# Feed-forwards: the sums of squares over the features as two products of 128 columns

## The chip, the core and the metric

One core of a Trainium2 chip. The metric is the device time of one execution in microseconds (us), median over several executions. Engines are named as in the profile: PE is TensorE's matmul, PEld its weight load, DVE is VectorE, ACT is ScalarE, POOL is GpSimd, SP is the engine that issues the DMAs.

## What is computed

Two layers of an encoder block and then two layers of a hybrid attention block, on one sequence of 256 tokens with 1024 features. Each encoder layer is a feed-forward, a mixer (stick-breaking attention beside a gated delta rule), a cross attention on a memory of 256 tokens, and a second feed-forward. All in float32.

```python
def rms_norm(x, gain, eps=RMS_EPS):
    xf = x.astype(F32)
    y = xf * lax.rsqrt(jnp.mean(xf * xf, axis=-1, keepdims=True) + eps)
    return (y * gain.astype(F32)).astype(x.dtype)

def swiglu_ffn(x, w_in, w_out):
    gate, up = jnp.split(x @ w_in, 2, axis=-1)
    return (jax.nn.silu(gate) * up) @ w_out

    for l in range(DEPTH):
        h = h + 0.5 * swiglu_ffn(rms_norm(h, ffn1_norm[l]), ffn1_w_in[l], ffn1_w_out[l])
        h = h + hybrid_mixer(rms_norm(h, mix_norm[l]), ...)
        h = h + memory_cross_attention(rms_norm(h, xattn_norm[l]), ...)
        h = h + 0.5 * swiglu_ffn(rms_norm(h, ffn2_norm[l]), ffn2_w_in[l], ffn2_w_out[l])
```

The width of a feed-forward is 2816, so the gate and the up projection have 22 tiles of 128 features each.

## The kernel before, in words

The state `h` lies with its features on the partitions: 8 tiles of 128 features by 256 tokens. Weights come as a stream of units of 8 blocks of 128 x 128 (512 KB each, 560 units) through a ring of six places (SP issues the DMAs). Each value is split into a high part, rounded to a shorter format, and a low part that holds the rest: ACT makes the high part of a weight unit (L1122), DVE the low part (L1556). A product of a weight tile is then three matmuls: high by high, high by low (both with the high weights as the stationary operand) and low by high. In `project` these are the lines L382, L385 and L386; in `first_pair`, which is the same for the first tile pair of a stage, L447, L451 and L452. The moving operand of each has 256 columns, one for each token. A tile pair (gate and up of one tile) is 48 matmuls.

The norm is applied late. The projections run on `h` times gain, and the factor 1/rms per token is multiplied onto the results by DVE (L1631 in a feed-forward). The factor is made beside the first projections: ACT squares `h`, DVE adds the eight tiles to `ssum` (128 partitions x 256 tokens), and TensorE adds over the partitions with a product against a matrix of ones. That is `token_sums`. It is float32 and not split. With `wide` it gives the sums as 128 equal rows of 256 tokens (L460: stationary `ones`, moving `ssum`, 256 columns), with `tall` as columns (L463, two products with `ssum` stationary and 2 columns moving, one for each half of the tokens). ACT then takes the logarithm and the exponential (L1136 and L1140), DVE waits for that (`x_rstd`).

Eight stages call it with `wide`: the four feed-forwards (`tall=False`), the two mixers and the two hybrid layers (both forms). The cross attentions ask for the tall form alone. In a feed-forward it stands in TensorE's order between the first tile pair and the 21 others; the result goes to bank 5, which no projection of the gate and up tiles uses (they go through banks 0 to 4). Behind those 21 x 48 matmuls come the 4 x 132 of the output projection, on the moving operand `a`, and then the first tile pair of the next stage.

TensorE works in program order. Other float32 products interrupt its stream of 256-column matmuls in the mixer: L549, L551 and L553 in `sums` (a constant stationary, 256, 128 and 128 columns), and L751, L759, L766 and L774 to L778 late in the delta rule (128 columns).

Of the kernel before, what the change touches and what calls it, by code (L numbers as in the profile page):

```python
# [29 lines left out]
P = 128  # L30
# [142 lines left out]
def build_program(nc, counts, arrays, out):  # L173
    with ExitStack() as ctx:
        def sb(name, *shape):
            return ctx.enter_context(nc.sbuf_tensor(name, [P, *shape], F32))
# [16 lines left out]
        bank = [banks[:, i, :] for i in range(8)]  # L193
# [12 lines left out]
        rstd, mrstd, ssum = sb("rstd", T)[:, :], sb("mrstd", T)[:, :], sb("ssum", T)[:, :]  # L206
# [3 lines left out]
        def C(name):  # L210
            return CONST(const, name)
# [12 lines left out]
        ident, ones, bones, le = C("ident"), C("ones"), C("bones"), C("le")  # L224
# [231 lines left out]
        def token_sums(pe, b, wide=True, tall=True, src=None):  # L456

            pe.e.wait_ge(*pe.need('x_ss', 0))
            if wide:
                last = nc.tensor.matmul(bank[b][:, 0:T], ones, ssum, start=True, stop=True, skip_group_check=True)  # L460
            if tall:
                for t in range(2):
                    last = nc.tensor.matmul(bank[b][:, T + 2 * t:T + 2 * t + 2], ssum[:, t * P:(t + 1) * P],  # L463
                        ones[:, 0:2], start=True, stop=True, skip_group_check=True)
            last.then_inc(*pe.tell('x_sum'))
# [28 lines left out]
        def ffn_pe(pe, w):  # L494
            with pe.scope("ffn"):
                first_pair(pe, w, xs, 0, "gu_full")
                pe.e.wait_ge(sems("loaded_const"), 16)
                token_sums(pe, 5, tall=False)
                for f in range(1, KF):
                    if f >= 5:  # L500
                        pe.e.wait_ge(*pe.need('ff', f - 4))
                    project(pe, w, xs, KD, f % 5, "gu_full")
                for b in FFN_BANKS:
                    project(pe, w, a_, KF, b, "down_full", "ff" if b == 5 else None)

        def mixer_pe(pe, w, l):
            with pe.scope("mix"):
                pe.e.wait_ge(sems("loaded_rest"), 48)
                first_pair(pe, w, xs, 0, "qk_full")
                token_sums(pe, 7)  # L510
                pe.e.wait_ge(*pe.need('m_ss', 0))
                nc.tensor.matmul(bank[6][:, 0:T], ones, mrstd, start=True, stop=True, skip_group_check=True)
# [280 lines left out]
        def cross_pe(pe, w):  # L793
            with pe.scope("cross"):
# [17 lines left out]

                first_pair(pe, w, yx, 0, "q_full")
                token_sums(pe, 6, wide=False)
                for i in range(XH + 2):
                    if i + 1 < XH:
# [1522 lines left out]
```

## Time and profile before

| | |
|---|---|
| median of 3 timed runs | 1859.49 us (1853.56 to 1860.68) |
| profiled execution | 1856.4 us |
| its span in the trace | 1854.6 us |
| PE busy | 1825.6 us, 98% |
| PEld busy | 1742.3 us, 94% |
| DVE busy | 1242.4 us, 67% |
| ACT busy | 978.3 us, 53% |
| granted TensorE clock, mean | 0.999 of 2.4 GHz |
| read from HBM | 299 MB, 162 GB/s over the span |

Times in the rows count from the start of the span. Matmuls overlap: a record of 281 ns begins some 118 ns after the one before it, so the busy time of PE doesn't tell its pace, the starts do. A float32 product leaves two matmul records and two weight loads, a split one leaves one for each matmul. The trace merges neighbours of one line into one row (x2, x4), whose duration goes from the first start to the last end.

### The profile page before, as it was taken

The numbers are of one execution on the slowest core, as the hardware profiler recorded it, in microseconds if no ns is written. First come the engines' busy times: TensorE is split into PE (matmuls) and PEld (weight loads), VectorE is DVE, ScalarE is ACT, GpSimd is POOL, SyncE is SP. The second block draws the span as 40 slices with busy tenths as digits, with TensorE's granted clock in tenths as the row PEclk, the third lists the DMA queues.
The fourth block names the chain that finished last, engine by engine and source line by source line (L and its number), as shares of the span: only waits on it lengthen the run. The fifth ranks groups of instructions, "written<-read, shape, count | busy, mean of one in ns | idle before, by whom it ended". The sixth has DMA issues, their size and how long they took to land.

```text
span 1854.6 us, 35725 instructions
## 1 busy us (share of the span) xinstructions
PE 1825.6 (98%) x15290; PEld 1742.3 (94%) x15290; DVE 1242.4 (67%) x1895; ACT 978.3 (53%) x1493; POOL 67.9 (4%) x32
## 2 busy tenths in 40 slices
PE   7999999999999999999999999999999999999999
PEld 7999998899999999999988999999989989989889
DVE  6775666765766567756667657665776678766676
ACT  6443567355544454445673555444555565656562
POOL 0000011400000000000114000000000000000000
PEclk9999999999999999999999999999999999999999
DMA  8555543233555655555432335555446334446332
GB/s 328 188 186 189 172 156 118 92 126 120 185 184 187 211 182 191 185 184 179 151 118 97 126 114 182 183 189 186 160 159 213 130 112 173 160 148 227 126 111 95
DMA packets 84461, 302.40 MB, mean 163 GB/s; under 512 B 9168, under 2 KB 11728, under 8 KB 84176
## 3 DMA queue, kind: packets, MB, share of 16 engines
q1 hardware_dynamic: 84304, 300.13, 46.4%
q8 instruction: 120, 1.97, 0.4%
q14 instruction: 37, 0.30, 0.1%
HBM read 299.04 MB, written 1.05 MB: 162 GB/s over the span
## 4 chain that ended last, share of the span: by engine, by line
PE 90%; DVE 5%; ACT 3%; issue 1%; DMA 0%; SPq 0%; DVEq 0%; ACTq 0%
PE bank L382 22%; PE bank L385 22%; PE bank L386 22%; PE bank L688 2%; DVE w_lo L1556 1%; PE bank L404 1%; PE bank L403 1%; PE bank L400 1%; PE bank L447 1%; PE bank L451 1%; PE bank L452 1%; PE bank L615 1%; PE bank L1005 1%; PE bank L1056 1%; PE bank L890 1%; PE bank L1026 1%
## 5 line engine op out<-in xcount | busy, mean ns | idle before, releaser
L1556 DVE TENSOR_TENSOR w_lo<-ring,w_hi 128x1024 fp32r<-128x1024 f32 x560 | 678.6, 1247 | 98.1 <-ACT w_hi L1122 97.0
L1122 ACT ACTIVATE w_hi<-ring 128x1024 fp32r<-128x1024 f32 x560 | 580.1, 1054 | 261.2 <-PE bank L382 222.1
L382 PE MATMUL bank<-xs,w_hi 128*128 128x256 f32 x2448 | 694.0, 284 | 0.0
L386 PE MATMUL bank<-xs,w_lo 128*128 128x256 f32 x2448 | 684.8, 280 | 0.0
L385 PE MATMUL bank<-xs,w_hi 128*128 128x256 f32 x2448 | 684.7, 280 | 0.0
L382 PEld LDWEIGHTS bank<-xs,w_hi 128*128 128x128 f32 x2448 | 463.5, 189 | 4.1 <-issue 3.0
L385 PEld LDWEIGHTS bank<-xs,w_hi 128*128 128x128 f32 x2448 | 462.1, 189 | 3.2 <-issue 2.9
L386 PEld LDWEIGHTS bank<-xs,w_lo 128*128 128x128 f32 x2448 | 462.4, 189 | 0.0
L382 PE MATMUL bank<-a,w_hi 128*128 128x256 f32 x704 | 197.8, 281 | 0.0
L385 PE MATMUL bank<-a,w_hi 128*128 128x256 f32 x704 | 197.8, 281 | 0.0
L386 PE MATMUL bank<-a,w_lo 128*128 128x256 f32 x704 | 197.8, 281 | 0.0
L382 PEld LDWEIGHTS bank<-a,w_hi 128*128 128x128 f32 x704 | 133.7, 190 | 0.0
L386 PEld LDWEIGHTS bank<-a,w_lo 128*128 128x128 f32 x704 | 132.9, 189 | 0.0
L385 PEld LDWEIGHTS bank<-a,w_hi 128*128 128x128 f32 x704 | 132.9, 189 | 0.0
L1631 DVE TENSOR_TENSOR arena<-bank,rstd 128x256 f32<-128x256 f32 x88 | 37.4, 425 | 140.7 <-PE bank L386 136.6
L1183 ACT ACTIVATE arena<-arena 128x256 f32<-128x256 f32 x88 | 36.9, 419 | 167.2 <-DVE arena L1631 167.2
L1595 DVE SCALAR_TENSOR_TENSOR arena<-bank,rstd 128x512 f32<-128x512 f32 (+1 forms) x20 | 11.7, 584 | 61.8 <-PE bank L386 61.8
L1152 ACT ACTIVATE xs<-h,enc_par 128x256 fp32r<-128x256 f32 x40 | 18.6, 505 | 57.3 <-DVE h L1598 44.2
L447 PE MATMUL bank<-xs,w_hi 128*128 128x256 f32 x128 | 37.4, 292 | 11.2 <-DVE w_lo L1556 9.8
L1304 ACT ACTIVATE arena<-bank 128x512 f32<-128x512 f32 x24 | 13.5, 597 | 60.8 <-PE bank L688 60.8
L400 PE MATMUL bank<-w_hi,xs 128*128 128x512 f32 (+2 forms) x128 | 43.3, 338 | 0.0
L404 PE MATMUL bank<-w_lo,xs 128*128 128x512 f32 (+2 forms) x128 | 42.9, 335 | 0.0
(399 smaller groups left out, 3086.2 us busy)
## 6 DMA issues: line engine op xcount, KB each, us to landing
ring<-in_w SPq DMA_DIRECT2D x560, 512.0 KB, 3.3
arena<-in_mem SPq DMA_DIRECT2D x2, 1024.0 KB, 12.8
const<-in_const SPq DMA_DIRECT2D x1, 1395.0 KB, 15.9
h<-in_x SPq DMA_DIRECT2D x1, 768.0 KB, 7.1
out<-h SPq DMA_DIRECT2D x3, 256.0 KB, 2.5
dec_par<-in_dec SPq DMA_DIRECT2D x1, 615.0 KB, 19.9
h<-in_x SPq DMA_DIRECT2D x1, 256.0 KB, 4.9
out<-h SPq DMA_DIRECT2D x2, 128.0 KB, 2.0
```

Of the source, the lines that this page charges most:

```text
L382: last = nc.tensor.matmul(o, wh, hi(x, k0 + k), start=k == 0, stop=False, skip_group_check=True)
L385: nc.tensor.matmul(o, wh, lo(x, k0 + k), start=False, stop=False, skip_group_check=True)
L386: last = nc.tensor.matmul(o, wl, hi(x, k0 + k), start=False, stop=k == nk - 1, skip_group_check=True)
L400: last = nc.tensor.matmul(o, xh, wh, start=k == 0, stop=False, skip_group_check=True)
L404: last = nc.tensor.matmul(o, xh, wl, start=False, stop=k == KD - 1, skip_group_check=True)
L447: last = nc.tensor.matmul(o, wh, hi(x, k), start=j == 0 and k == 0, stop=False, skip_group_check=True)
L688: last = nc.tensor.matmul(cut(bank[b], i)[o:o + n, o:o + n], x, y, start=True, stop=True, skip_group_check=True)
L1122: nc.scalar.activation(w_hi[:, s * UNIT:(s + 1) * UNIT], ring[:, u % RU, :], AF.Copy).then_inc(sems("w_hi"), 1)
L1152: nc.scalar.activation(hi(x, k), h[:, k, :], AF.Copy, scale=gain[:, k:k + 1]).then_inc(*a.tell('x_hi'))
L1183: nc.scalar.activation(e, e, AF.Silu).then_inc(*a.tell('ff_e'))
L1556: nc.vector.tensor_tensor(w_lo[:, r * UNIT:(r + 1) * UNIT], ring[:, r, :], w_hi[:, s * UNIT:(s + 1) * UNIT].bitcast(F32), ALU.subtract).th ...
L1631: nc.vector.tensor_tensor(ebuf[:, f % 5, :], bank[f % 5][:, 0:T], rstd, ALU.mult).then_inc(*d.tell('g_r'))
```

## The change

`token_sums` has a new branch for the case `wide` without `tall`, that is for the feed-forwards: two products of 128 columns, one for each half of the tokens, in place of one of 256. Both have the same stationary operand, and the last of them tells `x_sum`. The case `wide and tall` keeps the product of 256 columns, and the tall form is as it was.

```diff
         def token_sums(pe, b, wide=True, tall=True, src=None):
 
             pe.e.wait_ge(*pe.need('x_ss', 0))
-            if wide:
+
+            if wide and tall:
                 last = nc.tensor.matmul(bank[b][:, 0:T], ones, ssum, start=True, stop=True, skip_group_check=True)
+            elif wide:
+                for t in range(2):
+                    last = nc.tensor.matmul(bank[b][:, t * P:(t + 1) * P], ones, ssum[:, t * P:(t + 1) * P],
+                        start=True, stop=True, skip_group_check=True)
             if tall:
                 for t in range(2):
                     last = nc.tensor.matmul(bank[b][:, T + 2 * t:T + 2 * t + 2], ssum[:, t * P:(t + 1) * P],
```

## Rows read from the trace of the kernel before

**Rows 1.** The page: span, busy time by engine, granted clock by slice, chain by engine.
```profile
span 1854.6 us, 35725 instructions
...
PE 1825.6 (98%) x15290; PEld 1742.3 (94%) x15290; DVE 1242.4 (67%) x1895; ACT 978.3 (53%) x1493; POOL 67.9 (4%) x32
...
PEclk9999999999999999999999999999999999999999
...
PE 90%; DVE 5%; ACT 3%; issue 1%; DMA 0%; SPq 0%; DVEq 0%; ACTq 0%
```

**Rows 2.** Records of L460: ns min/median/max, first and last start; who waited.
```profile
L460 PE MATMUL bank<-ssum,const x16: 377/377/381, 18.2 to 1590.2; 128*128 128x256 f32 x16
...
  ACT rstd L1136: 0.6, 1
```

**Rows 3.** PE in order of time, first feed-forward: start us, us, line, form, count.
```profile
18.04 0.28 PE L452 MATMUL bank<-xs,w_lo 128*128 128x256 f32 x1
...
18.16 0.59 PE L460 MATMUL bank<-ssum,const 128*128 128x256 f32 x2
...
18.40 0.47 PE L382 MATMUL bank<-xs,w_hi 128*128 128x256 f32 x1
...
18.70 0.28 PE L385 MATMUL bank<-xs,w_hi 128*128 128x256 f32 x1
```

**Rows 4.** One line within a stretch: count, ns min/median/max, first and last start.
```profile
L385 PE MATMUL bank<-xs,w_hi x333: 281/281/281, 19.8 to 137.1; 128*128 128x256 f32 x167
...
L385 PE MATMUL bank<-xs,w_hi x31: 276/276/277, 864.5 to 874.7; 128*128 128x256 f32 x31
...
L452 PE MATMUL bank<-xs,w_lo x6: 276/276/276, 16.3 to 18.0; 128*128 128x256 f32 x6
...
L452 PE MATMUL bank<-xs,w_lo x16: 281/281/281, 475.9 to 481.2; 128*128 128x256 f32 x16
...
L452 PE MATMUL bank<-xs,w_lo x16: 281/281/281, 662.9 to 668.2; 128*128 128x256 f32 x16
...
L452 PE MATMUL bank<-xs,w_lo x10: 276/276/276, 1129.8 to 1132.9; 128*128 128x256 f32 x10
```

**Rows 5.** PE in order of time, first mixer, end of `sums`.
```profile
257.54 0.38 PE L551 MATMUL bank<-arena,const 128*128 128x128 f32 x2
257.76 0.39 PE L553 MATMUL bank<-arena,const 128*128 128x128 f32 x2
257.90 0.37 PE L382 MATMUL bank<-xs,w_hi 128*128 128x256 f32 x1
258.11 0.28 PE L385 MATMUL bank<-xs,w_hi 128*128 128x256 f32 x1
```

**Rows 6.** One line behind float32 products: after L553, L759 (twice), L1026 (twice).
```profile
L385 PE MATMUL bank<-xs,w_hi x15: 276/276/276, 258.5 to 263.2; 128*128 128x256 f32 x15
...
L735 PE MATMUL bank<-xs,w_lo x4: 276/276/278, 387.7 to 388.7; 128*128 128x256 f32 x4
...
L735 PE MATMUL bank<-xs,w_lo x4: 281/281/283, 1037.8 to 1038.9; 128*128 128x256 f32 x4
...
L386 PE MATMUL bank<-xs,w_lo x8: 280/281/281, 1782.1 to 1784.5; 128*128 128x256 f32 x8
...
L386 PE MATMUL bank<-xs,w_lo x8: 276/276/278, 1802.2 to 1804.6; 128*128 128x256 f32 x8
```

**Rows 7.** Weight loads in order of time, first mixer, at L463.
```profile
205.37 0.63 PEld L463 LDWEIGHTS bank<-const,ssum 128*128 128x128 f32 x4
```

**Rows 8.** Busy time by engine (count), clock, DMA share, GB/s in a feed-forward stretch.
```profile
700.00:740.00 40.00, 40.00 (x342) 40.00 (x341) 28.39 (x47) 20.51 (x29) 0.00 (x0) 1.00 0.52 185
```

**Rows 9.** The page: groups by line and form, count, busy us, mean ns.
```profile
L385 PE MATMUL bank<-xs,w_hi 128*128 128x256 f32 x2448 | 684.7, 280 | 0.0
...
L382 PE MATMUL bank<-a,w_hi 128*128 128x256 f32 x704 | 197.8, 281 | 0.0
```

## Prediction

> **What bounds the kernel now.** I read the page first. TensorE is busy for 98% of the span and the chain that ended last is TensorE for 90% of its length [rows 1]; the granted clock is at its upper level (2.4 GHz) in nearly every slice [rows 1]. So the time of this kernel is a count of matmuls times the distance from one start to the next, plus a few waits. DVE and ACT are beside it: in a feed-forward stretch of 40 us DVE works 28.39 us and ACT 20.51 us while TensorE never pauses [rows 8]. What happens to the four feed-forwards is therefore read from one thing, the distance between matmul starts.
>
> The changed products next. `token_sums` is called with `tall=False` only in `ffn_pe`, four times in the program. The records of L460 are sixteen in all, two for each of eight calls, 377 ns each [rows 2]: a float32 product is recorded as two passes. The four calls of the mixers and decoders (`wide and tall`) keep their form; the four of the feed-forwards change. One wait of 0.6 us is all that anybody spent on the result of L460 directly (ACT, before the logarithm) [rows 2].
>
> Then the pace of the stream of 256-column matmuls around it, which is the view that matters. In the first feed-forward, L385 has 333 records from 19.8 to 137.1 us, 281 ns each [rows 4]; two neighbours are three matmuls apart, so the pace is 117.3 / (332 x 3) = 0.1178 us a matmul. In a piece of the second mixer the same line, with the same shape and the same granted clock, has 31 records from 864.5 to 874.7 us of 276 ns: 10.2 / (30 x 3) = 0.1133 us [rows 4]. So there are two paces for the same work, 113.3 and 117.8 ns, and the duration of a record (276 or 281 ns) tells which one a stretch is in. All four feed-forwards run at the slow one from end to end (the first stands in the rows, the others repeat it); each has 1584 matmuls between the changed product and the sums of squares of the layer behind it (21 x 48 for gate and up, 4 x 132 for the output and 48 of the next layer's first pair).
>
> **Where the pace is decided.** In the first feed-forward the matmuls ahead of L460 are fast (L452, 276 ns, six records up to 18.0 us) and those behind it slow; the same in the fourth (276 ns up to 1132.9 us, slow behind). Ahead of the second and third call the stream is slow already (281 ns) and stays so [rows 4]. The timeline shows the restart: L460's two passes from 18.16, then L382 at 18.40 and L385 at 18.70 us, 0.30 us later, after which the slow pace holds [rows 3]. Following all starts through the trace, the pace never changes in the middle of an undisturbed stream; it changes only at a float32 product or at a wait that really stops TensorE. It is thus a position that the stream falls into at a restart, and the shape of the last product ahead of it has a say.
>
> **The change part by part.**
> It removes one float32 product of 256 columns per feed-forward: two records, each with its 256 columns streamed twice. They take 0.59 - 0.377 = 0.213 us from start to start [rows 2, 3], so 0.43 us.
> It adds two products of 128 columns with the same stationary operand. The nearest rows are L551 and L553 in the mixer: constant stationary, float32, 128 columns, two records each. L551 starts at 257.54 and L553 at 257.76, 0.22 us for one [rows 5], so 0.44 us for two: +0.01 us a call. From above: each record needs its own weight load, and in the neighbouring L463 four loads take 0.63 us, the last of them some 0.19 us of it (as long as the busy time of a load in the trace, which is 189 ns for the groups of L382), 0.147 us apart [rows 7]; four of them would be 0.59 us, +0.16 us. From below: 0, since the same columns are streamed. I take +0.01, the row nearest in form: for four calls +0.04 us, between 0 and +0.64.
> Waits: the same `x_ss` ahead, the same single `x_sum` at the end, at most 0.16 us later. Behind it ACT's logarithm and then DVE's first scaling have five banks of projections as cover, so nothing is paid there; without that cover it would be the 0.16 us. No DMA, no queue and no other engine gets anything new.
> The pace behind it: this is the term that decides. Where the stream restarts fast, 1584 matmuls save 0.1178 - 0.1133 = 4.5 ns each, 7.1 us per feed-forward, 28.5 us for four.
>
> **Does it restart fast?** After L549, L551, L553, that is after two products of 128 columns with a constant stationary operand, L382 and L385 follow at 257.90 and 258.11, 0.21 us apart and not 0.30 [rows 5], and the stream is fast (276 ns) [rows 6]; the trace has six such places and all six are fast. They had a 256-column product ahead of them and a fast stream before that. Over all places where 128-column float32 products directly precede the 256-column stream (44, the first at 257.90, the last at 1801.85 us), 35 restart fast and 9 slow; rows of both kinds stand in [rows 6], among them L759, fast in one layer (387.7 us) and slow in the other (1037.8 us). L759 with its neighbours L751, L766 and L774 to L778 speaks against the second and third call: where the stream ahead of them was already slow, four of five stayed slow; where it was fast, two of three restarted fast. Yet if the second call turns fast, the third is entered from a fast stream, since nothing in a feed-forward stops TensorE long enough to lose it. And the faster stream must be fed: DVE's 28.39 us per 40 [rows 8] become 29.5, still a quarter free.
>
> [...]
>
> **The cases.** The profiled execution lasts 1856.4 us (span 1854.6 and 1.8 around it), 3.1 below the median of the timed runs, 1859.5. The terms are differences, so I add them to the median.
> A, the forecast: all four feed-forwards run fast: 1859.5 - 28.5 + 0.04 = 1831.0 us (by the profiled execution 1827.9). Chance 0.42.
> B: two or three turn, for instance the first and fourth, which are entered fast, while the second and third stay as L759 at 1037.8 us did: -14.2 to -21.4, 1838 to 1845 us. For it speak the slow entries above; against it that the third inherits from the second. Chance 0.30.
> C: none or one turns, because the restart follows what came before and not the number of columns (or because there is one pace and what I read as two is something else in the feed-forwards): 1852.4 or 1859.5 us, up to 0.64 more by the weight loads. Chance 0.24.
> D, slower: the stretches outside the feed-forwards that are now fast turn slow, because everything behind the first changed product starts at another moment and every restart is drawn again. L385 on `xs` has 684.7 / 2448 = 279.7 ns in the mean where a wholly slow group (on `a`) has 281.0 [rows 9]; with 276 for fast that makes 26% of 3 x 2448, about 1900 matmuls, and 8.6 us if all of them turn, with 0.64 for the weight loads about 9.2 us: 1868.7. It decides only if no feed-forward gains and nearly all of these turn. Restarts by L551/L553 were fast in both layers, which speaks against it. Chance 0.04.
>
> **The numbers.** A difference under 0.5% (9.3 us) is about what a measurement of this kernel can't tell from none. A and B lie beyond it: faster 0.72; C within: same 0.24; slower 0.04. The range goes from 1826 (A with some 5 us of luck in the other restarts, the size of half of D's term) to 1855 (one feed-forward turned, with 2.6 us of the spread of the runs); it leaves out no gain at all (0.14) and D.
>
> **What would show it.** In the profile after: L460's successor with four records per feed-forward call about 0.11 us apart; L382 to L385 behind it 0.20 us apart, not 0.30; L385 and L386 in the four feed-forwards at 276 ns and 113.3 ns apart; the first feed-forward's stretch from the product to the mixer's L460, now 18.2 to 205.2 us, shorter by 7.1. If it shows 281 ns behind the new products, C is right. If DVE's w_lo or a DMA then stops TensorE within a feed-forward, the supply was the next bound and A loses part of its gain. What makes the prediction wrong is above all the step from the mixer's L553 to here.

## The result, and the profile after

| | before | after |
|---|---|---|
| median of 11 timed runs | 1856.96 us | 1844.92 us |
| lowest and highest | 1846.16, 1860.68 | 1834.28, 1850.34 |
| ratio, 95% interval | 1 | 0.9938, 0.9911 to 0.9964 |
| profiled execution, its span | 1856.4, 1854.6 us | 1844.92, 1843.1 us |

The changed kernel is faster by 0.6%, some 12 us. That is less than half of the 28.5 us that were forecast, and the executions of either kernel lie some 15 us apart. Ratios here and below leave out two single runs that lie far off, one of 5349.25 us of the kernel with four products and one of 2573.23 us of the kernel before.

First the page of after, its span and busy time by engine: the matmuls are the same but for eight records (15298 instead of 15290, [rows 1]), and PE's busy time is 12.0 us less.

```profile
span 1843.1 us, 35741 instructions
...
PE 1813.6 (98%) x15298; PEld 1730.4 (94%) x15298; DVE 1242.3 (67%) x1895; ACT 977.1 (53%) x1493; POOL 67.9 (4%) x32
```

Where it went, by the view of [rows 4]: L385 in the first, second, third and fourth feed-forward of after (count, ns min/median/max, first and last start).

```profile
L385 PE MATMUL bank<-xs,w_hi x334: 276/276/276, 19.8 to 133.0; 128*128 128x256 f32 x167
...
L385 PE MATMUL bank<-xs,w_hi x333: 276/276/276, 475.9 to 588.8; 128*128 128x256 f32 x167
...
L385 PE MATMUL bank<-xs,w_hi x333: 281/281/281, 656.0 to 773.3; 128*128 128x256 f32 x167
...
L385 PE MATMUL bank<-xs,w_hi x332: 281/281/281, 1120.9 to 1237.9; 128*128 128x256 f32 x166
```

Two of the four run at the fast pace, (588.8 - 475.9) / (332 x 3) = 0.1134 us a matmul, and two at the slow one, (773.3 - 656.0) / (332 x 3) = 0.1178. There are two paces indeed, and against this trace of before two of the four feed-forwards have gone from the slow one to the fast one. They aren't the ones that the reasoning of the prediction would pick. L452 ahead of the second, third and fourth call shows how each was entered:

```profile
L452 PE MATMUL bank<-xs,w_lo x13: 281/281/281, 470.0 to 474.2; 128*128 128x256 f32 x13
...
L452 PE MATMUL bank<-xs,w_lo x14: 276/276/276, 649.8 to 654.2; 128*128 128x256 f32 x14
...
L452 PE MATMUL bank<-xs,w_lo x11: 276/276/279, 1115.4 to 1118.8; 128*128 128x256 f32 x11
```

The second, entered slow, left fast. The third and the fourth, entered fast, left slow. (The first was entered slow, with the product 0.26 us behind the last matmul instead of 0.12, and left fast.) The restart itself is as foreseen, here the third call of after in order of time: L464 (the two new products, four records), then L382 and L385 0.20 us apart, as behind L553 [rows 5] and not 0.30 as in [rows 3].

```profile
654.22 0.28 PE L452 MATMUL bank<-xs,w_lo 128*128 128x256 f32 x1
654.34 0.60 PE L464 MATMUL bank<-ssum,const 128*128 128x128 f32 x4
654.70 0.36 PE L382 MATMUL bank<-xs,w_hi 128*128 128x256 f32 x1
654.90 0.28 PE L385 MATMUL bank<-xs,w_hi 128*128 128x256 f32 x1
```

The four records begin (0.60 - 0.28) / 3 = 0.11 us apart. From L464 to L382 it is 0.36 us, where [rows 3] has 0.24 from L460 to L382; L385 follows 0.56 instead of 0.54 us behind the product's start. So the new products cost 0.02 us a call.

### The profile page after: what moved, and what is told of

It is laid out like the page before. It is cut to its first block, busy times and chain, and to the rows that moved or that the text cites. A ratio compares the mean times of both kernels' runs of the same rounds, so it can differ in the third digit from the quotient of the medians.

```text
span 1843.1 us, 35741 instructions
## 1 busy us (share of the span) xinstructions
PE 1813.6 (98%) x15298; PEld 1730.4 (94%) x15298; DVE 1242.3 (67%) x1895; ACT 977.1 (53%) x1493; POOL 67.9 (4%) x32
## 4 chain that ended last, share of the span: by engine, by line
PE 90%; DVE 5%; ACT 3%; issue 1%; DMA 0%; SPq 0%; DVEq 0%; ACTq 0%
PE bank L382 22%; PE bank L386 22%; PE bank L385 22%; PE bank L693 2%; DVE w_lo L1561 1%; PE bank L404 1%; PE bank L403 1%; PE bank L400 1%; PE bank L447 1%; PE bank L451 1%; PE bank L452 1%; PE bank L620 1%; PE bank L1010 1%; PE bank L1061 1%; PE bank L895 1%; PE bank L1031 1%
## 5 line engine op out<-in xcount | busy, mean ns | idle before, releaser
L382 PE MATMUL bank<-xs,w_hi 128*128 128x256 f32 x2448 | 691.8, 283 | 0.0
L385 PE MATMUL bank<-xs,w_hi 128*128 128x256 f32 x2448 | 682.6, 279 | 0.0
L385 PEld LDWEIGHTS bank<-xs,w_hi 128*128 128x128 f32 x2448 | 465.1, 190 | 3.0 <-issue 2.9
L382 PEld LDWEIGHTS bank<-xs,w_hi 128*128 128x128 f32 x2448 | 462.2, 189 | 3.9 <-issue 2.7
L382 PE MATMUL bank<-a,w_hi 128*128 128x256 f32 x704 | 196.1, 278 | 0.0
L385 PE MATMUL bank<-a,w_hi 128*128 128x256 f32 x704 | 196.1, 278 | 0.0
L385 PEld LDWEIGHTS bank<-a,w_hi 128*128 128x128 f32 x704 | 133.7, 190 | 0.0
L382 PEld LDWEIGHTS bank<-a,w_hi 128*128 128x128 f32 x704 | 132.2, 188 | 0.0
L447 PE MATMUL bank<-xs,w_hi 128*128 128x256 f32 x128 | 37.0, 289 | 11.6 <-DVE w_lo L1561 10.2
```

The source lines that it names most:

```text
L382: last = nc.tensor.matmul(o, wh, hi(x, k0 + k), start=k == 0, stop=False, skip_group_check=True)
L385: nc.tensor.matmul(o, wh, lo(x, k0 + k), start=False, stop=False, skip_group_check=True)
L447: last = nc.tensor.matmul(o, wh, hi(x, k), start=j == 0 and k == 0, stop=False, skip_group_check=True)
```

## The experiments

The theory, named P in the expectations: there are two positions in which the stream of matmuls can run, it holds the one it has until a float32 product or a real stop of TensorE interrupts it, and where it restarts depends on how it stood when the interruption began and on how long the interruption is, counted in records. The rival R is that the shape of the last product decides, with some chance.

**Once more, the changed kernel**, with no edit.

> The changed kernel once more, for a second trace. Theory P (position): the pace behind the sums is set by where the stream of matmuls stands when the float32 products begin. Entered at the fast pace (113.3 ns) it leaves two products of 128 columns at the slow one (117.8 ns), as the third and fourth feed-forward did; entered at the slow pace it can leave at either. So each feed-forward is wholly fast (179.6 us from restart to the next sums) or wholly slow (186.6 us), none in between, and every one entered fast is slow. Rival R (shape): the number of columns decides with some luck, and then a feed-forward entered fast is as often fast as slow.

Measured 1850.68 us, span 1848.9. One feed-forward is fast, the second: entered slow, left fast, as in the first trace. The three others were entered fast and all three are slow. L452 ahead of the third call and L385 behind it:

```profile
L452 PE MATMUL bank<-xs,w_lo x16: 276/276/276, 656.3 to 661.4; 128*128 128x256 f32 x16
...
L385 PE MATMUL bank<-xs,w_hi x332: 281/281/281, 663.7 to 780.7; 128*128 128x256 f32 x166
```

Whole feed-forwards, none mixed: from the restart to the next sums 179.62 us at the fast pace, 186.64 to 186.65 at the slow one. That is what P says, but the first counts for little: there TensorE stood still for the sum ahead of L464 (0.98 us from start to start), so its entry was no longer that of a running stream. The difference to the profiled execution of after, 5.8 us in the span, is one feed-forward (7.0) less 1.5 us behind the last of them.

**A third product.**

```diff
                 for t in range(2):
                     last = nc.tensor.matmul(bank[b][:, t * P:(t + 1) * P], ones, ssum[:, t * P:(t + 1) * P],
                         start=True, stop=True, skip_group_check=True)
+                for t in range(1):
+                    last = nc.tensor.matmul(bank[b][:, T + t * P:T + (t + 1) * P], ones, ssum[:, t * P:(t + 1) * P],
+                        start=True, stop=True, skip_group_check=True)
```

> A third float32 product of 128 columns in each feed-forward, behind the two, into the unused half of the bank (its result is read by nobody). Theory P: each record of such a product moves the restart by the same small step, two records more put a stream that was entered fast into another position, which I expect to be a fast one: entered fast, it leaves fast, so the third feed-forward follows the second and the fourth is fast too; three or four feed-forwards at 113.3 ns, some 7 to 14 us below the changed kernel (1831 to 1838 us) though each has 0.22 us more work. Rival R (shape): a third product of the same shape changes nothing but 4 x 0.22 us: as the changed kernel, 1846 us.

Measured 1835.51 us (1829.73 to 1839.31), ratio 0.9891 (0.9856 to 0.9925) to before. More work and less time. The third call in order of time, and then L385 in the third and the fourth feed-forward of this kernel:

```profile
661.35 0.28 PE L452 MATMUL bank<-xs,w_lo 128*128 128x256 f32 x1
661.47 0.60 PE L464 MATMUL bank<-ssum,const 128*128 128x128 f32 x4
661.91 0.39 PE L467 MATMUL bank<-ssum,const 128*128 128x128 f32 x2
662.05 0.37 PE L382 MATMUL bank<-xs,w_hi 128*128 128x256 f32 x1
```

```profile
L385 PE MATMUL bank<-xs,w_hi x331: 276/276/276, 664.0 to 776.2; 128*128 128x256 f32 x166
...
L385 PE MATMUL bank<-xs,w_hi x330: 276/276/276, 1121.9 to 1233.8; 128*128 128x256 f32 x165
```

Both were entered fast (L452 ahead of the third call: 276 ns, 14 records up to 661.4 us) and left fast; with two products both had left slow. The second, entered slow, left fast. The first, entered slow and with a stop of TensorE ahead of the products (1.21 us from start to start), left slow.

**Four products.** The same loop with `range(2)`.

> Two more float32 products of 128 columns in each feed-forward, four in all (the last two are read by nobody). Theory P: records of such products follow each other 111.67 ns apart in the mean, so four of them take 446.7 ns, and positions repeat after four records: a feed-forward entered fast leaves four products as it leaves two, slow. Then as the changed kernel plus 4 x 0.45 us, 1847 us. If three products give fast and four slow, it is position and not number. Rival R (shape): as the changed kernel plus 1.8 us as well, but with fast and slow behind any entry. Rival M (more float32 work always makes a fast restart likelier): four is at least as good as three, 1832 us.

Measured a median of 1851.19 us, ratio 0.9957 (0.9929 to 0.9986): no better than the changed kernel. L452 ahead of the third call, then L385 in the third and the fourth feed-forward:

```profile
L452 PE MATMUL bank<-xs,w_lo x16: 276/277/277, 657.2 to 662.3; 128*128 128x256 f32 x16
...
L385 PE MATMUL bank<-xs,w_hi x332: 280/281/282, 664.9 to 781.8; 128*128 128x256 f32 x166
...
L385 PE MATMUL bank<-xs,w_hi x332: 280/281/282, 1129.8 to 1246.7; 128*128 128x256 f32 x166
```

Entered fast and slow again, as with two. So three help and four don't. The rival that more float32 work helps (M) is out, and so is the shape of the last product as the only cause, since it is the same with two, three and four. A position that comes round again after four records, as P has it, foretold this.

**A third product of 2 columns.**

```diff
+                last = nc.tensor.matmul(bank[b][:, T:T + 2], ones, ssum[:, 0:2], start=True, stop=True,
+                    skip_group_check=True)
```

> The third product of e2 with 2 columns in place of 128 (sums of two tokens, read by nobody). The records of L463, with 2 columns, follow each other as those of 128 columns do, 0.11 us apart, since the weight load sets the distance. Theory P: what counts is how many such records stand there, six, not how many columns they stream: entered fast, it leaves fast, as with the third product of 128 columns; 1831 to 1840 us. Rival R (shape, the last product must have 128 columns): as with two products or worse; entered fast it leaves slow, 1846 to 1855 us.

Measured 1833.52 us (1828.92 to 1836.73), ratio 0.9881 (0.9845 to 0.9917). L385 in the fourth feed-forward, entered fast:

```profile
L452 PE MATMUL bank<-xs,w_lo x14: 276/276/281, 1113.9 to 1120.0; 128*128 128x256 f32 x14
...
L385 PE MATMUL bank<-xs,w_hi x330: 276/276/276, 1123.0 to 1234.8; 128*128 128x256 f32 x165
```

Fast. Two columns did what 128 do: either product leaves two records, and from the first product to the restart it took 0.58 us with either. It is one such entry in one trace, but the median too lies where P put it (1831 to 1840 us) and not where R did (1846 to 1855). R, that the last product must have 128 columns, is out. (The third feed-forward is fast here too, though it was entered slow, and the second stayed slow: behind a slow entry either can come.)

**The sums without a float32 product.** The edit stands against the products of the changed kernel:

```diff
-                for t in range(2):
-                    last = nc.tensor.matmul(bank[b][:, t * P:(t + 1) * P], ones, ssum[:, t * P:(t + 1) * P],
-                        start=True, stop=True, skip_group_check=True)
+                nc.tensor.matmul(bank[b][:, 0:T], ones_r[:, 0:P], ssum_hi[:, :], start=True, stop=False, skip_group_check=True)
+                last = nc.tensor.matmul(bank[b][:, 0:T], ones_r[:, 0:P], ssum_lo[:, :], start=False, stop=True,
+                    skip_group_check=True)
```

and on DVE, behind the last addition:

```diff
+                d.e.wait_ge(*d.own())
+                nc.vector.tensor_copy(ssum_hi[:, :], ssum).then_inc(*d.tell())
+                d.e.wait_ge(*d.own())
+                nc.vector.tensor_tensor(ssum_lo[:, :], ssum, ssum_hi[:, :].bitcast(F32), ALU.subtract).then_inc(*d.tell('x_ss'))
```

Not shown: `ones_r`, a rounded copy of the ones that DVE makes once at the start, and the places of the new tiles.

> The sums of squares of the four feed-forwards without a float32 product: DVE splits the sum into a high and a low part, and TensorE adds each over the partitions with a rounded matrix of ones, two matmuls of 256 columns that have the form of the stream around them. Theory P: without a float32 product nothing restarts the stream, so the pace of the first tile pair carries through the whole feed-forward: entered fast, it stays fast for all 1584 matmuls; entered slow, it stays slow, and the third has the pace of the second. In the traces so far the fourth was entered fast and the second slow; so one or two of four fast, 1842 to 1850 us. Rival R (it is something in the feed-forward itself, the operands or the supply of weights, that keeps it slow): slow in all four, 1859 us.

Measured 1848.18 us, ratio 0.997 (0.9945 to 0.9994). Two feed-forwards were fast, which the number foresaw, but not the way: the third was entered fast, nothing stopped it, and it left slow. In order of time, then L457 (the L452 of this kernel) ahead of it and L390 behind:

```profile
655.70 0.28 PE L457 MATMUL bank<-xs,w_lo 128*128 128x256 f32 x1
655.81 0.28 PE L468 MATMUL bank<-ssum_r,ones_r 128*128 128x256 f32 x1
655.93 0.28 PE L469 MATMUL bank<-ssum_r,ones_r 128*128 128x256 f32 x1
656.05 0.28 PE L387 MATMUL bank<-xs,w_hi 128*128 128x256 f32 x1
```

```profile
L457 PE MATMUL bank<-xs,w_lo x16: 275/277/277, 650.6 to 655.7; 128*128 128x256 f32 x16
...
L390 PE MATMUL bank<-xs,w_hi x331: 280/281/282, 657.9 to 774.5; 128*128 128x256 f32 x166
```

So part of the theory falls: it need not be a float32 product or a stop. Two matmuls of the stream's own form that read other tiles, 0.12 us apart, were enough to lose the fast position (one case). The expectation had the fourth entered fast; here it was entered slow and left slow. The first left fast behind a stop (1.13 us from start to start, for DVE's added steps); the second was entered slow and left fast, and there the sum came a little late too (from L468 to the restart 0.26 us, where the third took 0.24). R of this run, that something in the feed-forward itself keeps it slow, is out.

**The kernel before, once more**, with no edit.

> The kernel before once more, for a second trace. Theory P (position): one float32 product of 256 columns, entered fast, leaves at the slow pace, as in the first and fourth feed-forward of the first trace; entered slow it stayed slow twice of twice. So every feed-forward that is entered fast takes 186.7 us; at most one entered slow may turn out fast, and at most two are fast (the second hands its pace to the third only if the product lets it, and it doesn't). Rival C (chance at every restart): two or more fast ones, also behind a fast entry.

Measured 1844.62 us, span 1842.8: two feed-forwards fast in the kernel before itself, the first and the third. The expectation that every feed-forward entered fast takes 186.7 us held for the fourth and failed for the first: there TensorE had stopped for the sum, from the last L452 at 17.80 to L460 at 18.78 us, and behind a stop either pace came: this first feed-forward left fast and that of the changed kernel's second trace slow, each entered fast and 0.98 us from start to start.

```profile
17.80 0.28 PE L452 MATMUL bank<-xs,w_lo 128*128 128x256 f32 x1
18.78 0.67 PE L460 MATMUL bank<-ssum,const 128*128 128x256 f32 x2 [0.70 <-DVE ssum L1584]
19.10 0.47 PE L382 MATMUL bank<-xs,w_hi 128*128 128x256 f32 x1
19.41 0.28 PE L385 MATMUL bank<-xs,w_hi 128*128 128x256 f32 x1
```

```profile
L385 PE MATMUL bank<-xs,w_hi x329: 275/276/277, 21.8 to 133.3; 128*128 128x256 f32 x165
```

The third was entered slow and left fast, which the first trace had not shown. So the kernel before has none in one trace and two in the other, 11.8 us apart in the span, which is most of the width of its 11 runs (1846 to 1861 us). The prediction rests on a trace with none. Behind a fast entry without a stop the change gains nothing: one product of 256 columns left slow there, as two of 128 do.

**Another place for xs.** The changed kernel with `xs` 64 bytes further.

```diff
+        sb("xs_pad", 16)
         xs_at = here()
```

> The changed kernel with the tile xs, the moving operand of all projections except the output ones of the feed-forwards (those read a), 64 bytes further in SBUF; everything else, a included, keeps its place modulo 128 bytes. It asks what the two paces are made of. Theory P alone says nothing on the address: the same two paces, 113.3 and 117.8 ns, each carried through a feed-forward, 1844 to 1850 us. Rival A (the pace depends on how the two operands lie to each other in SBUF): the stretches on xs get another pace than those on a within one feed-forward, and a stream doesn't keep one pace from L386 on xs to L386 on a; then by the two thirds of the matmuls that read xs the time moves by more than 1%.

Measured 1873.26 us (1872.06 to 1874.54), ratio 1.0114 (1.0076 to 1.0153). Its groups in a stretch of the first feed-forward (line, form, count, busy us, mean ns):

```profile
L386 PE MATMUL bank<-xs,w_hi 128*128 128x256 f32 x329 | 93.1, 283 | 0.0
...
L386 PE MATMUL bank<-a,w_hi 128*128 128x256 f32 x176 | 48.6, 276 | 0.0
```

A third pace, 283 ns a record and by the starts 120.0 ns from one to the next, on `xs`, and the fast one on `a`, within one undisturbed stream and the same in all four feed-forwards. Rival A is right, and P has to be completed: where the moving operand lies in SBUF decides which paces there are. With `xs` at 64 modulo 128 bytes, where `a` lies in every kernel here, there are the two of 113.3 and 117.8 ns; at 0 modulo 128 there was only that of 120.0. (Not everything else kept its place, as the expectation has it: the edit moves the tiles between `xs` and the arena as well, `sq`, the sums and the parameters, by the same 64 bytes. The matmuls of the two streams read none of them.) What in the reading of the two operands makes the paces isn't shown by any run here.

**Three products again, and twice three.** The kernel with three products, and one with three more behind the second tile pair:

```diff
                     project(pe, w, xs, KD, f % 5, "gu_full")
+                    if f == 1:
+                        for t in (0, 1, 0):
+                            nc.tensor.matmul(bank[6][:, t * P:(t + 1) * P], ones, ssum[:, t * P:(t + 1) * P],
+                                start=True, stop=True, skip_group_check=True)
```

> The kernel with three products of 128 columns again, to weigh it against the one before with more rounds. Theory P: the first feed-forward is entered at either pace from a stall at the start and is fast in part of the executions; the second, third and fourth fast in most. Median 1832 to 1838 us, ratio to before 0.985 to 0.991, executions some 7 us apart from each other. If the first result was luck: ratio 0.994 as for the changed kernel.

Measured 1837.11 us (1831.38 to 1842.72), ratio 0.9909 (0.9881 to 0.9936). In the profiled execution, the fastest of them, all four feed-forwards are fast.

> As the kernel with three products of 128 columns, and three more of them behind the second tile pair of each feed-forward (into a bank that is not in use; read by nobody), 0.7 us more work each, 2.8 us in all. Theory P: a stream that is fast when it meets them leaves them fast, so they cost only their 0.7 us; one that is slow enters from another position and has a new chance. All four feed-forwards fast in more executions, the spread between executions smaller, lowest execution 1832, median 1834 to 1837 us. Rival: three products behind a fast stream leave it slow as often as not; then a fast feed-forward turns slow behind its second tile pair, and the median is 1845 us or more.

Measured 1833.76 us (1831.96 to 1836.16), ratio 0.9891 (0.9862 to 0.9921). In its trace the first feed-forward was slow behind the first three products and fast behind the second three; the others were fast behind the first and stayed so. (The first had been entered fast, but the sum came late there: the first load of L464 began 0.04 us behind its turn, and from L464 to the restart it took 0.62 us instead of 0.58.) L385 in the first, between the two groups and behind them:

```profile
L385 PE MATMUL bank<-xs,w_hi x15: 281/281/281, 19.8 to 24.8; 128*128 128x256 f32 x15
...
L385 PE MATMUL bank<-xs,w_hi x309: 276/276/276, 29.9 to 134.6; 128*128 128x256 f32 x155
```

> The kernel with three products, and three more behind the second tile pair, again, with more rounds. Theory P: all feed-forwards fast in nearly every execution, so 28.5 us less than with none and 2.8 + 0.9 us of added work: ratio to before 0.987 to 0.991, median 1833 to 1837 us, and a smaller spread than the kernel before (its executions lie over 18 us). If the first result was luck: median near 1845 us.

Measured 1832.89 us (1832.28 to 1834.48, six runs), ratio 0.9898 (0.9865 to 0.9931). All four feed-forwards are fast behind the second restart in both traces, and the spread is 2.2 us (4.2 in the round above) where the runs of before beside them lay from 1841.84 to 1861.65. This version beats the kernel before by 1.0%. Against the changed one it is 0.4% going by the two ratios (0.9898 and 0.9938), whose intervals overlap and which were not measured side by side. It does so with 3.6 us of work that computes nothing (0.22 us a call for the third product and 0.67 for the second group). L385 in its first and fourth feed-forward:

```profile
L385 PE MATMUL bank<-xs,w_hi x308: 276/276/276, 29.8 to 134.2; 128*128 128x256 f32 x154
...
L385 PE MATMUL bank<-xs,w_hi x297: 276/276/276, 1129.8 to 1230.5; 128*128 128x256 f32 x149
```

All runs with a trace in one table; S is slow, F fast, for the first to the fourth feed-forward:

| kernel | paces | span us |
|---|---|---|
| before, first trace | S S S S | 1854.6 |
| before, second | F S F S | 1842.8 |
| changed, first | F F S S | 1843.1 |
| changed, second | S F S S | 1848.9 |
| four products | S F S S | 1849.8 |
| split sums | F F S S | 1840.6 |
| three products | S F F F | 1837.5 |
| third of 2 columns | F S F F | 1834.9 |
| three, again | F F F F | 1829.5 |
| twice three, two traces | F F F F | 1831.3, 1831.0 |

Left out is the kernel with `xs` moved. From none to four feed-forwards at the fast pace the span falls by 25.1 us, 6.3 for each.

Sorted by entry, the same traces say what the products do. Behind a fast entry with nothing late, one product of 256 columns left slow in 3 of 3 cases, two products of 128 slow in 4 of 4, three products (the one with 2 columns and the second groups counted in) fast in 16 of 16, four slow in 2 of 2. Behind a slow entry either pace came; the second feed-forward, which was entered slow in every kernel, left fast in 0 of 2 traces with one product, 2 of 2 with two, 4 of 5 with three and 1 of 1 with four. No run delays the stream by a chosen time and leaves the products alone, so that it is the moment of the restart that counts is inferred from this order, and not shown by itself.

## Why the prediction was right in part and wrong in size

**What bounds the kernel**: right. The stream of matmuls does, and its pace is a state that a whole feed-forward keeps.

**The cost of the edit**: right. +0.01 us a call was forecast, +0.02 found; the bound of 0.16 from the weight loads of L463 wasn't needed.

**What one feed-forward gains**: right. 7.1 us forecast; 186.75 us from restart to the next sums in the trace of before, 179.62 at the fast pace in after, 7.1. (The Trainium skill, "TensorE: Matmul & The Clock Gate", section Back-to-back issue gap, gives N / 2.4 plus 2.5 ns for a matmul on its own, which is 109 ns at 256 columns; no stream here ran at that, the lowest pace is 113.3 ns. For a stream of weight loads and matmuls it gives some 81 ns at 128 columns and 131 ns at 512, one value each. The streams here, with 256 columns, lie between the two and have more than one value.)

**How many gain**: here it failed. The step was "does it restart fast?", which took the six fast places behind L551 and L553 as the nearest row. They have the same form of product, but ahead of them stands L549 with 256 columns, so the stream comes to the two products in another position. The row was chosen by the shape of the products, when what counts is the entry and the number of records behind it: entered fast without a stop, two products of 128 columns left slow in every feed-forward of the changed kernel's two traces where that can be read (third and fourth in both), three left fast and four slow. The term of 28.5 us was to be 14.3. The prediction gave that its own case (B, 1838 to 1845 us, 0.30), and named for instance the first and the fourth as the two that would turn, because they are entered fast; it was the other way round, entered slow the second left fast, entered fast the third and the fourth left slow. That the first did turn is luck: it was entered slow this time, and the product came late.

How much of the gain is the edit's doing is open in part. Behind a fast entry it gains nothing, since one product of 256 columns leaves slow there too. The second feed-forward is the only one that is slow in both traces of before and fast in both of after. Its 7.1 us would make a ratio of 0.9962, just inside the measured interval; the medians lie 12.0 us apart. Where the rest comes from the traces don't show. That the two profiled executions differ by 11.5 us, close to the medians, is partly luck: the second trace of before has two fast feed-forwards and that of after has one.

**The rest of the difference**: two fast feed-forwards are 14.3 us, the four restarts cost 0.1 us in all; 11.5 us are in the span. The missing 2.7 us lie nearly all behind the last feed-forward. From the sums behind it to the end it takes 534.6 us before and 537.15 after. This is that stretch of after, and ten microseconds of it (us, busy by engine and count, granted clock, DMA share, GB/s):

```profile
1305.95:1843.10 537.15, 527.79 (x4264) 490.06 (x4262) 375.98 (x606) 296.93 (x531) 0.00 (x0) 0.99 0.45 149
1430.00:1440.00 10.00, 8.17 (x59) 8.07 (x58) 4.49 (x9) 4.35 (x6) 0.00 (x0) 0.83 0.35 107
```

TensorE's clock fell to its lower level (1.2 GHz) for 3.4 us at 1435 us, an idle time of 1.83 us having ended at 1434.5, and twice more in the second hybrid layer, at 1654 and 1705; in the 5 to 7 us ahead of the three it was busy for 3.67 us of 5.50, 6.90 of 6.90 and 3.27 of 5.10. In the trace of before it fell once, at 1449. Over the traces (all but that with `xs` moved) the stretch is 532.6 us long with no time at the lower clock, 534.6 to 535.2 with 3.4 us of it (five traces), 535.7 to 536.3 with 6.8 us (three), and 537.2 and 538.2 with 10.2 us. It comes and goes between executions of one kernel and is no work of the change.

**Case D**, the restarts elsewhere drawn anew: nothing of 9 us. The mixers and cross attentions took 276.4 and 277.9 us before and 276.2 and 278.0 after.

**The chances**: faster had 0.72 and came. The measured median, 1844.92, is 13.9 us above the forecast of 1831.0. The drop that was forecast, 28.5, was 16.4 us more than the 12.0 measured; the median of before that the sum started from, 1859.5, stood 2.5 us above that of eleven runs, which hid that much of it.

## What to carry to other kernels

Where TensorE's stream bounds a kernel, read the distance between starts (and whether the duration of one form has two values) stage by stage before anything else: 4% of pace over 1584 matmuls was worth 7.1 us here, where the work of the edit itself came to 0.02. A pace that is a state isn't predicted by the shape of the last edit; look for places in the trace that are entered in the same state and have the same number of records behind the entry, and, if none is there, give the mixed case most of the chance. And if a state is at stake, one trace of a kernel is one draw: the two traces of the kernel before have none and two fast feed-forwards.

## What the runs showed of the hardware that was not expected

The same matmul at the same granted clock has three paces here: 113.3, 117.8 and 120.0 ns from start to start (records of 276, 281 and 283 ns), the last with `xs` moved by 64 bytes.

The starts of a fast stream lie on a grid. 113.33 ns is 17 times 6.667, and in the slow stream three matmuls take 353.3 ns, 53 times 6.667; four records of 128-column float32 products take 4 x 111.67 = 446.7, 67 times. Take the starts of the weight loads modulo 6.667 ns (with a drift of 1.6 ns per millisecond taken out). In the eleven traces with `xs` in its place, 2021 of 2028 stretches of 30 loads at the fast pace then stand within 0.35 ns of one place of their trace, whatever lies between them.

Where a restart falls on this grid goes with the pace. The count is over the 469 restarts behind four or more float32 records of up to 128 columns that have no wait at them or behind them and at least 20 matmuls of the stream to follow, each measured from that place to the second weight load behind the products. Of those between 5.5 and 6.667 or up to 0.2 ns, 139 came out fast and 1 slow; between 3.3 and 4.4 ns 116 fast and 1 slow; between 2.0 and 2.7 ns 1 fast and 37 slow; of the rest 135 fast and 39 slow. (The bounds were chosen with the result in view.) Two records more shift a restart by 3.3 ns. In the feed-forwards that were entered fast, two products stand at 2.4 (slow), three at 5.5 to 6.1 (fast), four at 1.7 and 2.7 (slow). What has this period isn't shown.
